# Two PSUM banks for the scan's diagonal, the cb tiles in SBUF, and TensorE's program written out for both layers

## The chip, the core and the metric

One core of one Trainium2 chip runs the whole kernel in a single launch. The time is device microseconds from start to end; the median of several executions counts. In the profile PE is TensorE's matmuls and PEld its weight loads, DVE is VectorE, ACT is ScalarE, POOL is GpSimd and SP is SyncE, which here only starts DMAs. A "q" behind an engine (DVEq) is its sequencer: drains, waits, register work.

## What is computed

An encoder of two layers on 256 tokens of width 1024, float32. The reference, cut down:

```python
for i in range(DEPTH):                       # DEPTH = 2
    h = rms_norm(x, mix_norm_g[i])
    proj = h @ w_in[i]                       # q, k, v, z, xBC, dt, memory q, 3 gates
    y_da  = diff_attention(q, k, v, ...)     # 8 heads
    y_ssm = mamba2_bidir(z, xBC, dt, ...)    # 32 heads, 4 groups, forward and backward scan
    y_xa  = mem_cross_attention(xq, rms_norm(mem), w_mem_kv[i])
    merged = g0 * (y_da @ wb_da) + g1 * (y_ssm @ wb_ssm) + g2 * (y_xa @ wb_xa)
    x = x + merged @ w_out[i]
    h = rms_norm(x, ffn_norm_g[i])
    gate, up = split(h @ w_ffn_in[i])
    x = x + (silu(gate) * up) @ w_ffn_out[i]
return rms_norm(x, final_norm_g)

# one direction of the scan, chunks of 128 tokens:
cb = einsum('bclgn,bcsgn->bcgls', Cc, Bc)                 # per group
m = cb * segsum_exp(a)                                    # decay between tokens
y_diag = einsum('bcgrls,bcsgrp->bclgrp', m, xdt)          # inside a chunk
y_off  = einsum(Cc, state of the other chunk) * exp(a_cs) # between chunks
```

## The kernel before

**Weights in units.** All large matrices stream through one ring of four slots. A unit is 128 x 1024 numbers of a weight (two blocks of 128 rows, 512 columns); a layer has 220 of them, numbered 0 to 219, and `GROUPS` lists to which product each group of units belongs. Every number is split into a high part and a rest, so that fast float32r matmuls give float32 results. For each unit SP loads `w_raw`, ScalarE casts the high part `wH` (line 896), VectorE, or for some units GpSimd, forms `wL` = `w_raw` - `wH` (line 1258, or 1191), and TensorE makes 12 to 24 matmuls from it (line 596), into the banks PS0 and PS1. An engine's step for unit u casts unit u + 3; so the operands of a unit are asked for three units ahead. While the input projections run ("mixing", units 26 to 125) all `wL` are VectorE's.

**Side work.** Everything else (norms, attention, convolution, scan) is cut into small steps. `layer_plan` gives each a unit number and an engine; `each_step` writes, for every engine, unit 0, its steps, unit 1, its steps and so on. Every engine runs its own list in order and meets the others at semaphores alone. The small matmuls and transposes write four side banks S0 to S3 of PSUM. `take(lay, bank)` makes TensorE wait until the bank's last reader has added to `side_free[bank]`; `side_uses` holds how often a layer takes each bank. TensorE can do nothing for the next unit while a side step waits.

**The scan.** 16 ticks i (4 groups g x 2 chunks c x 2 halves of the heads). The names and where they stand, x being the unit of tick i, 67 + 3i in the first layer's numbering:

- `conv`, `conv_silu`: convolution on VectorE (lines 1476, 1482), silu on ScalarE (1079), per block of 512 channels; `xs_turn` (TensorE, 797) transposes the result into bank 3, `xs_copy` (ScalarE, 1084) takes it out and frees the bank.
- `cb` (TensorE): B and C of group g, 256 x 256 numbers, into bank g % 2. `cb_rows` (ScalarE, 1107) copies the middle 256 columns of 512, the blocks between different chunks, to SBUF as `cboff`. The two diagonal blocks stay in the bank.
- `diff` (VectorE, 1544 and 1546) at x - 2, `decay_exp` (ScalarE, 1110) at x, `decay` (VectorE, 1554) at x + 3: the decay times cb's diagonal block, read from the bank. The last of four frees it.
- `diag` (TensorE) at x + 6: the tick's product, into bank 2. A chunk k has two ticks; the first takes the bank.
- `weigh`, `skip` (GpSimd, 1205 and 1213), `off` (TensorE, bank 3, reads `cboff`).
- `join` (VectorE): off's bank 3 times a gain (1564), plus diag's bank 2 (1567), and its drain (1568) frees bank 2. It stands one unit ahead of the diag of the next chunk. `gated` (1572, 1577) finishes the chunk in SBUF.
- `ssm_norm`, `ssm_turn` (TensorE, 854), `ssm_high` (ScalarE, 1124), `ssm_low` (VectorE, 1266): norm and transpose of the result; the first five transposes use bank 0.

Ahead of the scan come `dt_sums` (sums of dt by TensorE, which need VectorE's `aL`), the second half of the attention heads (`da_scores`, `da_exp`, `da_combine`, `da_turn`, line 769, and so on) and `cb_prod` (VectorE, 1526) with `cb_diag` (TensorE, sixteen matmuls of one column a layer in the trace) for the skip gain.

**Loops.** Each engine's program for a layer stands in one loop over both layers, and eight of its feed-forward groups in an inner loop. For TensorE this is

```python
            with pe.Fori(0, DEPTH) as lay:
```

at line 864; with `lay` in a register, each semaphore value it waits for is computed by register instructions.

## Time and profile before

| | |
|---|---|
| median of 3 executions | 1512.65 us (1511.44 to 1516.13) |
| profiled execution, its own time | 1514.97 us |
| its span, first to last instruction | 1513.1 us |
| TensorE matmuls, weight loads | busy 95%, 85% |
| VectorE, ScalarE, GpSimd | busy 63%, 53%, 24% |
| granted TensorE clock, mean | 0.986 of full |
| chain that ended last | TensorE 70%, VectorE 13%, its sequencer 8%, ScalarE 4% |

A busy TensorE here means matmuls that overlap: one of 512 columns is shown with 389 ns, and they start 227 ns apart. So the share says little on how much can be gained; the stops do, and the clock. Each view below is of this one execution. Layer 1 lasts to 760 us, layer 2 to some 1500 us, and the scan of layer 1 lies between about 264 and 475 us.

### The profile page before, as it was taken

The numbers are of one execution on the slowest core, as the hardware profiler recorded it, in microseconds if no ns is written. First come the engines' busy times: TensorE is split into PE (matmuls) and PEld (weight loads), VectorE is DVE, ScalarE is ACT, GpSimd is POOL, SyncE is SP. The second block draws the span as 40 slices with busy tenths as digits, with TensorE's granted clock in tenths as the row PEclk, the third lists the DMA queues.
The fourth block names the chain that finished last, engine by engine and source line by source line (L and its number), as shares of the span: only waits on it lengthen the run. The fifth ranks groups of instructions, "written<-read, shape, count | busy, mean of one in ns | idle before, by whom it ended". The sixth has DMA issues, their size and how long they took to land.

```text
span 1513.1 us, 25594 instructions
## 1 busy us (share of the span) xinstructions
PE 1443.5 (95%) x8905; PEld 1285.0 (85%) x8921; DVE 950.1 (63%) x1294; ACT 807.5 (53%) x1221; POOL 363.7 (24%) x170
## 2 busy tenths in 40 slices
PE   5999999999899999999999999999998999999997
PEld 5899888877777889999889988878786778899986
DVE  5354756989987446654433447588899864565543
ACT  5455577655555446444444546756556454544444
POOL 2310000110113344445333000001110134444443
PEclk9999999999999999999999999999999999999999
DMA  6564444665655564656555544446665556556564
GB/s 211 169 173 132 121 129 123 182 194 170 179 182 165 174 190 150 194 186 221 177 173 150 160 124 124 126 128 208 187 187 166 166 170 183 167 179 190 173 227 149
DMA packets 158500, 255.55 MB, mean 169 GB/s; under 512 B 12729, under 2 KB 58923, under 8 KB 158379
## 3 DMA queue, kind: packets, MB, share of 16 engines
q1 hardware_dynamic: 156427, 252.41, 55.3%
q10 hardware_dynamic: 1952, 1.61, 0.3%
q8 instruction: 66, 1.08, 0.3%
q14 instruction: 55, 0.45, 0.1%
HBM read 252.80 MB, written 1.18 MB: 168 GB/s over the span
## 4 chain that ended last, share of the span: by engine, by line
PE 70%; DVE 13%; DVEq 8%; ACT 4%; issue 3%; ACTq 1%; DMA 1%
PE PS L596 62%; PE S L596 6%; DVE wL L1258 5%; DVEq L1545 2%; DVEq L1479 2%; ACT wH L896 1%; PE S L603 1%; DVE actLf L1482 1%; DVE regA L1546 1%; DVEq L1558 1%; DVE regA L1544 1%; ACT scr L1045 1%; DVE regA L1554 1%; DVE scr L1567 1%; DMA rows<-in_ssm_D_dram 1%
## 5 line engine op out<-in xcount | busy, mean ns | idle before, releaser
L896 ACT CAST wH<-w_raw 128x1024 fp32r<-128x1024 f32 x443 | 458.2, 1042 | 550.6 <-PE PS L596 541.4
L1258 DVE TENSOR_TENSOR wL<-w_raw,wH 128x1024 fp32r<-128x1024 f32 (+1 forms) x322 | 438.3, 1363 | 406.4 <-ACT wH L896 392.1
L596 PE MATMUL PS<-hH,wH 128*128 128x256 f32 x1472 | 423.4, 288 | 0.0
L596 PE MATMUL PS<-hH,wL 128*128 128x256 f32 x1472 | 418.1, 284 | 0.0
L596 PE MATMUL PS<-hL,wH 128*128 128x256 f32 x1472 | 418.1, 284 | 0.0
L1191 POOL TENSOR_TENSOR wL<-w_raw,wH 128x1024 fp32r<-128x1024 f32 (+1 forms) x121 | 304.9, 2520 | 415.4 <-ACT wH L896 415.0
L596 PEld LDWEIGHTS PS<-hH,wH 128*128 128x128 f32 x1472 | 284.1, 193 | 4.3 <-issue 4.0
L596 PEld LDWEIGHTS PS<-hL,wH 128*128 128x128 f32 x1472 | 284.1, 193 | 0.3
L596 PEld LDWEIGHTS PS<-hH,wL 128*128 128x128 f32 x1472 | 283.9, 193 | 0.0
L596 PE MATMUL PS<-wH,actH 128*128 128x512 f32 x560 | 223.5, 399 | 0.0
L596 PE MATMUL PS<-wL,actH 128*128 128x512 f32 x560 | 219.2, 391 | 0.0
L596 PE MATMUL PS<-wH,actL 128*128 128x512 f32 x560 | 219.1, 391 | 0.0
L596 PE MATMUL PS<-wH,hH 128*128 128x512 f32 (+1 forms) x416 | 165.9, 399 | 0.0
L596 PE MATMUL PS<-wL,hH 128*128 128x512 f32 (+1 forms) x416 | 160.0, 385 | 0.0
L596 PE MATMUL PS<-wH,hL 128*128 128x512 f32 (+1 forms) x416 | 159.9, 384 | 0.0
L1205 POOL TENSOR_TENSOR regA<-actHf,dts 128x512 f32<-128x512 f32 x8 | 9.5, 1191 | 603.0 <-ACTq L1085 603.0
L596 PEld LDWEIGHTS PS<-wL,actH 128*128 128x128 f32 x560 | 105.7, 189 | 22.8
L596 PEld LDWEIGHTS PS<-wH,actL 128*128 128x128 f32 x560 | 106.0, 189 | 20.9
L596 PEld LDWEIGHTS PS<-wH,actH 128*128 128x128 f32 x560 | 106.0, 189 | 20.8
L596 PEld LDWEIGHTS PS<-wL,hH 128*128 128x128 f32 x416 | 79.3, 191 | 16.0
L596 PEld LDWEIGHTS PS<-wH,hH 128*128 128x128 f32 x416 | 79.6, 191 | 15.2 <-issue 1.3
L596 PEld LDWEIGHTS PS<-wH,hL 128*128 128x128 f32 x416 | 79.5, 191 | 14.2
(239 smaller groups left out, 1561.0 us busy)
## 6 DMA issues: line engine op xcount, KB each, us to landing
w_raw<-in_w_in_dram SPq DMA_DIRECT2D x192, 512.0 KB
w_raw<-in_w_ffn_in_dram SPq DMA_DIRECT2D x176, 256.0 KB
w_raw<-in_w_branch_dram SPq DMA_DIRECT2D x64, 512.0 KB
w_raw<-in_w_ffn_out_dram SPq DMA_DIRECT2D x44, 512.0 KB
w_raw<-in_w_mem_kv_dram SPq DMA_DIRECT2D x35, 512.0 KB
regA<-cs_rows SPq DMA_DIRECT2D x64, 256.0 KB, 4.5
w_raw<-in_w_out_dram SPq DMA_DIRECT2D x16, 512.0 KB
regA<-in_mem_dram SPq DMA_DIRECT2D x6, 512.0 KB, 5.4
```

The lines of the kernel that those rows point to most:

```text
L596: return nc.tensor.matmul(o, l, r, start=first, stop=last, skip_group_check=True)
L603: ins = nc.tensor.transpose(dst[:, at:at + P], src(t, k), ident[:, :])
L896: nc.scalar.copy(wH[:, slot].rearrange("p k c -> p (k c)")[:, q], raw[:, slot].rearrange("p k c -> p (k c)")[:, q]).then_inc(h_done[slot], 1)
L1045: ins = nc.scalar.activation(sc[b][:, T * q:T * (q + 1)], S[q // 2][:, T * (q % 2):T * (q % 2 + 1)], ACT.Exp, bias=nmx[b][:, q:q + 1], sca ...
L1191: nc.gpsimd.tensor_tensor(wL[:, slot].rearrange("p k c -> p (k c)")[:, q], raw[:, slot].rearrange("p k c -> p (k c)")[:, q], wH[:, slot].r ...
L1258: v.tensor_tensor(wL[:, slot].rearrange("p k c -> p (k c)")[:, q], raw[:, slot].rearrange("p k c -> p (k c)")[:, q], wH[:, slot].rearrange ...
L1479: dve.drain()
L1482: ins = v.scalar_tensor_tensor(tile[:, j, :], cin[:, j, k:k + T], p_cw[:, q:q + 1], tile[:, j, :], ALU.mult, ALU.add)
L1544: v.tensor_tensor(side, side, gains(cs[:, q:q + 4], 4, P), ALU.subtract)
L1545: dve.drain()
L1546: v.copy_predicated(b, upR[:, :].bitcast(U32).unsqueeze(1).broadcast_to([P, 4, P]), f)
L1554: ins = v.tensor_tensor(e, e, S[g % 2][:, (T + P) * c:(T + P) * c + P].unsqueeze(1).broadcast_to([P, 4, P]), ALU.mult)
```

## The change

1. TensorE's loop over the layers is a Python loop: its program stands there twice (6849 rows of instructions where there were 3658), with semaphore values as constants. The inner feed-forward loop stays, and so do the layer loops of the other engines.
2. `diag` takes banks 2 and 1 in turn, chunk by chunk.
3. `cb` takes bank 0 only; `cb_rows` copies all 512 columns to SBUF, drains and frees the bank. `decay` and `off` read that copy. The two copies lie in `scr` where `yN[0]` was; the tile `cboff` is gone.
4. `xs_turn` uses bank 0 instead of 3.
5. The plan's numbers: `dt_sums` to `cs_base` one unit later; attention heads 4 to 7 one unit earlier; `cb_diag` two units behind `cb_prod` instead of one; the scan's ticks one unit later; `xs_turn` two units apart and one or more later; `ssm_turn` 0 to 3 at ticks 41, 43, 45, 47 instead of 37, 39, 41, 43, counted from a start that is itself one later.

```diff
-    put(u + 6, "pe", "dt_sums")
+    put(u + 7, "pe", "dt_sums")
...
-        u = (first("xbc", 4) + 1 if half == 0 else first("v", 1) + 2) + 3 * j
+        u = (first("xbc", 4) + 1 if half == 0 else first("v", 1) + 1) + 3 * j
...
-    x = [first("xbc", 0) + 9 + 3 * i for i in range(4 * SG)]
-    u = first("xbc", 5) + 10
+    x = [first("xbc", 0) + 10 + 3 * i for i in range(4 * SG)]
+    u = first("xbc", 5) + 11
     put(u, "dve", "cb_prod")
-    put(u + 1, "pe", "cb_diag")
+    put(u + 2, "pe", "cb_diag")
...
-    for r, (turn, split) in enumerate(((37, 38), (39, 40), (41, 42), (43, 44), (59, 60), (59, 61), (60, 62), (60, 63))):
+    for r, (turn, split) in enumerate(((41, 42), (43, 44), (45, 46), (47, 48), (59, 60), (59, 61), (60, 62), (60, 63))):
...
-                put(u + 5 + (b == 0) + t, "pe", "xs_turn", 2 * b + t)
-                put(u + 6 + (b == 0) + t, "act", "xs_copy", 2 * b + t)
+                put(u + 6 + 2 * t, "pe", "xs_turn", 2 * b + t)
+                put(u + 7 + 2 * t, "act", "xs_copy", 2 * b + t)
...
-        cboff = [v3(t, NT) for t in (scr[:, 6144:6400], cboff_t[:, :])]
+        cb = [scr[:, 2560:3072], scr[:, 3072:3584]]
...
                 elif kind == "xs_turn":
-                    take(lay, 3)
+                    take(lay, 0)
...
                 elif kind == "cb":
-                    take(lay, i % 2)
+                    take(lay, 0)
...
                 elif kind == "diag":
                     g, c, hf = tick(i)
+                    bank = 2 - i // 2 % 2
                     if hf == 0:
-                        take(lay, 2)
+                        take(lay, bank)
...
-            with pe.Fori(0, DEPTH) as lay:
+            for lay in range(DEPTH):
...
                 elif kind == "cb_rows":
                     if i >= 2:
                         act.wait_ge(off_done, 8 * lay + 2 * i - 2)
-                    nc.scalar.copy(cboff[i % 2], v3(S[i % 2][:, P:P + T], 2)).then_inc(cb_ready, 1)
+                        act.wait_ge(m_done, 16 * lay + 4 * i - 4)
+                    nc.scalar.copy(cb[i % 2], S[0][:, :]).then_inc(side_free[0], 1)
+                    act.drain().then_inc(cb_ready, 1)
...
-                    ins = v.tensor_tensor(e, e, S[g % 2][:, (T + P) * c:(T + P) * c + P].unsqueeze(1).broadcast_to([P, 4, P]),
-                                          ALU.mult)
-                    if i % 4 == 3:
-                        ins.then_inc(side_free[g % 2], 1)
+                    v.tensor_tensor(e, e, cb[g % 2][:, (T + P) * c:(T + P) * c + P].unsqueeze(1).broadcast_to([P, 4, P]),
+                                    ALU.mult)
```

Two places show how this moves instructions. The names in square brackets are the semaphores waited for. First TensorE in the first layer, behind unit 103, at diag 10, before (`ssm_m` says that decay 10 is done) and after:

```order
2259 L592 REGISTER_ALU
2260 L842 REGISTER_ALU [waits xs_ready,side_free2]
2261 L596 MATMUL S<-actHf,regA 128x64 [waits ssm_m]
2262 L596 MATMUL S<-actHf,regA 128x64 x3
2263 L664 REGISTER_ALU
2264 L596 MATMUL PS<-wH,actH 128x512 [waits l_done0]
```

```order
2125 L595 MATMUL PS<-wL,actH 128x512
2126 L595 MATMUL S<-actHf,regA 128x64 [waits ssm_m,xs_ready,side_free1]
2127 L595 MATMUL S<-actHf,regA 128x64 x3
2128 L595 MATMUL PS<-wH,actH 128x512 [waits l_done1]
2129 L595 MATMUL PS<-wH,actL 128x512
```

The product now waits for the bank of two chunks ago, a unit later in the plan (the next unit's slot is 1, not 0), and the register instructions are gone.

Second VectorE, its units 111 to 114 in the first layer. Each `wL` row opens a unit; L1266 with `ssm_gh` is an ssm_low, L1554 a decay, L1564 with L1567 a join, L1326 the sum of a branch. Before:

```order
471 L1258 TENSOR_TENSOR wL<-w_raw,wH 128x1024 [waits h_done2]
472 L1266 SCALAR_TENSOR_TENSOR actL<-S,lp,actH 128x128 [waits ssm_gh]
473 L1266 SCALAR_TENSOR_TENSOR actL<-S,lp,actH 128x128 x3
474 L1258 TENSOR_TENSOR wL<-w_raw,wH 128x1024 [waits h_done3]
475 L1552 REGISTER_ALU
476 L1554 TENSOR_TENSOR regA<-regA,S 128x512 [waits ssm_exp]
477 L1257 REGISTER_ALU
478 L1258 TENSOR_TENSOR wL<-w_raw,wH 128x1024 [waits h_done0]
479 L1318 REGISTER_ALU
480 L1326 SCALAR_TENSOR_TENSOR scr<-scr,PS 128x1024 [waits unit_used1,psum_free1]
481 L1258 TENSOR_TENSOR wL<-w_raw,wH 128x1024 [waits h_done1]
482 L1564 TENSOR_TENSOR scr<-S,dts 128x512 [waits ssm_off]
```

And after, the lines counted one higher:

```order
468 L1259 TENSOR_TENSOR wL<-w_raw,wH 128x1024 [waits h_done3]
469 L1267 SCALAR_TENSOR_TENSOR actL<-S,lp,actH 128x128 [waits ssm_gh]
470 L1267 SCALAR_TENSOR_TENSOR actL<-S,lp,actH 128x128 x3
471 L1258 REGISTER_ALU
472 L1259 TENSOR_TENSOR wL<-w_raw,wH 128x1024 [waits h_done0]
473 L1319 REGISTER_ALU
474 L1327 SCALAR_TENSOR_TENSOR scr<-scr,PS 128x1024 [waits unit_used1,psum_free1]
475 L1553 REGISTER_ALU
476 L1555 TENSOR_TENSOR regA<-regA,scr 128x512 [waits ssm_exp]
477 L1259 TENSOR_TENSOR wL<-w_raw,wH 128x1024 [waits h_done1]
478 L1267 SCALAR_TENSOR_TENSOR actL<-S,lp,actH 128x128 [waits ssm_gh]
479 L1267 SCALAR_TENSOR_TENSOR actL<-S,lp,actH 128x128 x3
```

Decay 14 has moved behind the branch's sum, from unit 112 to 113, and reads `scr` instead of S; the join of unit 114 has given its place to the third ssm_low, which stood at unit 109, and follows one unit later.

## Rows read from the trace of the kernel before

**Rows 1.** The page: busy tenths of VectorE in 40 slices

```profile
DVE  5354756989987446654433447588899864565543
```

**Rows 2.** Writers of S, layer 1: what ended TensorE's idle time, us, times

```profile
  DVEq L1568: 9.9, 4
  ACT actHf L1084: 2.9, 4
  DVEq L1451: 2.2, 2
  DVEq L1587: 1.5, 1
  DVE aL L1265: 1.0, 1
  DVE regA L1526: 0.8, 1
```

**Rows 3.** The same view, layer 2, 830:1255 us: its largest difference from layer 1

```profile
  DVEq L1451: 2.3, 2
```

**Rows 4.** Timeline of TensorE: start us, us, work, idle before

```profile
265.58 0.63 PE L769 MATMUL S<-ident,scr 128*128 128x128 f32 x4 [1.65 <-DVEq L1451]
...
412.26 0.43 PE L596 MATMUL S<-actHf,regA 128*128 128x64 f32 x2 [4.75 <-DVEq L1568]
...
457.34 0.43 PE L596 MATMUL S<-actHf,regA 128*128 128x64 f32 x2 [1.07 <-DVEq L1568]
...
762.72 0.38 PE L596 MATMUL PS<-actH,wH 128*128 128x256 f32 x1 [2.06 <-issue]
```

**Rows 5.** Instructions of line 864: duration ns min/median/max, first and last start

```profile
L864 PEldq COMPARE_BRANCH  x2: 78/2918/5758, 756.5 to 1499.8; - x2
```

**Rows 6.** Stretches: busy us (x) of each engine, PEclk, DMA share, GB/s

```profile
268.00:274.00 6.00, 6.00 (x25) 4.97 (x25) 5.61 (x11) 0.37 (x1) 0.00 (x0) 0.72 0.53 141
...
411.00:418.00 7.00, 5.73 (x22) 4.62 (x23) 6.10 (x11) 1.21 (x2) 0.00 (x0) 0.76 0.40 107
763.00:769.00 6.00, 6.00 (x40) 6.00 (x40) 0.85 (x1) 3.22 (x9) 2.08 (x1) 0.72 0.50 162
1152.00:1161.00 9.00, 5.48 (x19) 4.75 (x20) 8.21 (x13) 2.27 (x2) 0.00 (x0) 0.62 0.27 76
```

**Rows 7.** Groups of VectorE, 264:449 us: busy, mean ns, idle before, releasers

```profile
L1258 DVE TENSOR_TENSOR wL<-w_raw,wH 128x1024 fp32r<-128x1024 f32 x50 | 63.7, 1276 | 12.8 <-ACT wH L896 8.2 <-issue 1.8
```

**Rows 8.** Timeline of ScalarE and VectorE at the scan's door

```profile
259.25 1.28 ACT L1079 ACT_TABLE_LOAD   x1
260.55 1.06 ACT L1079 ACTIVATE regA<-regA 128x1024 f32<-128x1024 f32 x1
...
262.84 1.23 DVE L1258 TENSOR_TENSOR wL<-w_raw,wH 128x1024 fp32r<-128x1024 f32 x1 [4.53 <-ACT wH L896]
```

**Rows 9.** Timeline of VectorE around ends of its units

```profile
414.24 1.22 DVE L1258 TENSOR_TENSOR wL<-w_raw,wH 128x1024 fp32r<-128x1024 f32 x1
...
444.80 1.12 DVE L1266 SCALAR_TENSOR_TENSOR actL<-S,lp,actH 128x128 fp32r<-128x128 f32 x4
...
450.95 1.22 DVE L1326 SCALAR_TENSOR_TENSOR scr<-scr,PS 128x1024 f32<-128x1024 f32 x1 [1.65 <-PE PS L596]
452.31 3.47 DVE L1258 TENSOR_TENSOR wL<-w_raw,wH 128x1024 fp32r<-128x1024 f32 x1
455.70 0.68 DVE L1564 TENSOR_TENSOR scr<-S,dts 128x512 f32<-128x512 f32 x1
...
457.30 1.45 DVE L1258 TENSOR_TENSOR wL<-w_raw,wH 128x1024 fp32r<-128x1024 f32 x1
...
1200.58 1.46 DVE L1258 TENSOR_TENSOR wL<-w_raw,wH 128x1024 fp32r<-128x1024 f32 x1
```

**Rows 10.** Instructions of lines 1554 and 1572: duration ns min/median/max

```profile
L1554 DVE TENSOR_TENSOR regA<-regA,S x32: 674/685/690, 289.9 to 1203.6; 128x512 f32<-128x512 f32 x32
...
L1572 DVE TENSOR_TENSOR scr<-scr x16: 676/685/2933, 323.4 to 1221.4; 128x512 f32<-128x512 f32 x16
```

More of the change, by code:

```diff
@@ L140, in layer_plan @@
     put(u + 5, "dve", "dt_out")
-    put(u + 6, "pe", "dt_sums")
-    put(u + 7, "dve", "dt_cs")
-    put(u + 8, "pe", "cs_turn")
-    put(u + 9, "act", "dt_decay")
-    put(u + 9, "dve", "dt_wgt")
-    put(u + 10, "act", "cs_store")
-    put(u + 11, "dve", "cs_base")
+    put(u + 7, "pe", "dt_sums")
+    put(u + 8, "dve", "dt_cs")
+    put(u + 9, "pe", "cs_turn")
+    put(u + 10, "act", "dt_decay")
+    put(u + 10, "dve", "dt_wgt")
+    put(u + 11, "act", "cs_store")
+    put(u + 12, "dve", "cs_base")
     for h in range(XH):
@@ L177, in layer_plan @@
                 put(u + 11 + 2 * q, "dve", "da_low", 2 * half + q)
-    x = [first("xbc", 0) + 9 + 3 * i for i in range(4 * SG)]
-    u = first("xbc", 5) + 10
+    x = [first("xbc", 0) + 10 + 3 * i for i in range(4 * SG)]
+    u = first("xbc", 5) + 11
     put(u, "dve", "cb_prod")
-    put(u + 1, "pe", "cb_diag")
-    put(u + 2, "dve", "d_gain")
+    put(u + 2, "pe", "cb_diag")
+    put(u + 3, "dve", "d_gain")
     for g in range(SG):
@@ L209, in layer_plan @@
     for n, b in enumerate(CONV_ORDER):
-        u = first("xbc", b) + (4 if b == 5 else 6 if b == 0 else 5)
+        u = first("xbc", b) + (4 if b == 5 else 7 if b == 0 else 5)
         for q in range(4):
@@ L257, in pool_splits @@
     return u % 2 == 1 and not mixing
-SIDE_USES = [23, 20, 33, 28]
+SIDE_USES = [33, 22, 29, 20]
 PAR_LOADS, ROW_LOADS = 7, 7
@@ L295, in build @@
         upR, loR, onesR = (sb(n, P, F32R) for n in ("upR", "loR", "onesR"))
-        cboff_t = sb("cboff", T)
         cs_rows = nc.dram_tensor("cs_rows", (NT, 2 * SH, P), F32, kind="Internal").ap()
@@ L796, in step @@
                     for j in range(4):
-                        ins = nc.tensor.transpose(S[3][:, P * j:P * (j + 1)], conv_tile(n)[:, j, P * t:P * (t + 1)],
+                        ins = nc.tensor.transpose(S[0][:, P * j:P * (j + 1)], conv_tile(n)[:, j, P * t:P * (t + 1)],
                                                   ident[:, :])
@@ L827, in step @@
                     for c in range(NT):
-                        ins = mm(S[i % 2][:, T * c:T * (c + 1)], BT[:, i, P * c:P * (c + 1)], CT[:, i, :], True, True)
+                        ins = mm(S[0][:, T * c:T * (c + 1)], BT[:, i, P * c:P * (c + 1)], CT[:, i, :], True, True)
                     ins.then_inc(cb_done, 1)
@@ L834, in step @@
                     pe.wait_ge(cb_ready, SG * lay + i // 2 + 1)
-                    mm(S[3][:, :], cboff[i // 2 % 2][:, 1 - c, :], xw[i % 2], True, True).then_inc(off_done, 1)
+                    mm(S[3][:, :], cb[i // 2 % 2][:, P * (2 - c):P * (3 - c)], xw[i % 2], True, True).then_inc(off_done, 1)
                 elif kind == "diag":
                     g, c, hf = tick(i)
+                    bank = 2 - i // 2 % 2
                     if hf == 0:
-                        take(lay, 2)
-                    if hf == 0:
+                        take(lay, bank)
                         pe.wait_ge(xs_ready, 8 * lay + 2 * g + c + 1)
@@ L844, in step @@
                         h = 4 * hf + j
-                        ins = mm(S[2][:, DH * h:DH * (h + 1)], RB[i % len(RB)][:, j, :],
+                        ins = mm(S[bank][:, DH * h:DH * (h + 1)], RB[i % len(RB)][:, j, :],
                                  xsN[g][:, c, DH * h:DH * (h + 1)], h == 0, True)
@@ L1083, in step @@
                     act.wait_ge(xs_turned, 8 * lay + i + 1)
-                    nc.scalar.copy(xsN[b][:, t, :], S[3][:, :]).then_inc(side_free[3], 1)
+                    nc.scalar.copy(xsN[b][:, t, :], S[0][:, :]).then_inc(side_free[0], 1)
                     act.drain().then_inc(xs_ready, 1)
@@ L1550, in step @@
                     if i % 4 == 0:
-                        dve.wait_ge(cb_done, SG * lay + g + 1)
+                        dve.wait_ge(cb_ready, SG * lay + g + 1)
                     dve.wait_ge(exp_done, 16 * lay + i + 1)
                     e = RB[i % len(RB)]
-                    ins = v.tensor_tensor(e, e, S[g % 2][:, (T + P) * c:(T + P) * c + P].unsqueeze(1).broadcast_to([P, 4, P]),
-                                          ALU.mult)
-                    if i % 4 == 3:
-                        ins.then_inc(side_free[g % 2], 1)
+                    v.tensor_tensor(e, e, cb[g % 2][:, (T + P) * c:(T + P) * c + P].unsqueeze(1).broadcast_to([P, 4, P]),
+                                    ALU.mult)
                     dve.drain().then_inc(m_done, 1)
@@ L1566, in step @@
                     dve.wait_ge(diag_done, 16 * lay + 2 * i + 2)
-                    v.tensor_tensor(ytmp, ytmp, S[2][:, :], ALU.add)
-                    dve.drain().then_inc(side_free[2], 1)
+                    bank = 2 - i % 2
+                    v.tensor_tensor(ytmp, ytmp, S[bank][:, :], ALU.add)
+                    dve.drain().then_inc(side_free[bank], 1)
                 elif kind == "gated":
```

## The prediction

> **What bounds the kernel now.** TensorE is busy in nine tenths of nearly every slice, so I read first why it stops at all. The view of the instructions that write the side banks S, one layer at a time, says what its idle time in front of them ended on: 18.7 us per layer, of which 9.9 us in four waits for VectorE's join (line 1568) and 2.9 us in four waits for ScalarE's copy out of bank 3 (line 1084) [rows 2, 3]. One wait stands outside the layers: 2.06 us that ended on nothing but issue [rows 4], at the branch of the layer loop. That branch row lasts 5.8 us where it is taken and 0.08 us where it falls through [rows 5].
>
> Second, the granted clock. Several stops are followed by a stretch at 1.2 GHz. A stretch costs its length times what is missing from full clock: 6 x 0.28 = 1.7 us at 268:274, 7 x 0.24 = 1.7 us at 411:418, 6 x 0.28 = 1.7 us at 763:769, 9 x 0.38 = 3.4 us at 1152:1161 [rows 6]. Layer 1 has three such stretches behind side work (the third, at 319:325, like the first), layer 2 has two, both like the last.
>
> Third, who is late where TensorE waits. VectorE's tenths in slices 8 to 12 are 9, 8, 9, 9, 8 [rows 1]; from 264 to 449 us its largest group waited only 8.2 us for ScalarE's halves, 4.5 of them in the first wait [rows 7]. What VectorE does not fill with counted work there are drains behind its own instructions. So in the scan TensorE waits for an engine that has no rest itself. The waits can be taken away; the time of VectorE can't.
>
> **The change, part by part.** I count in units: a layer has 220 weight units, TensorE takes about 2.9 us for one, and each engine's side steps hang behind its unit. A shift is how much earlier TensorE finishes a unit than before.
>
> *Layer loop written out.* The 2.06 us go [rows 4], and so does the slow stretch behind them, 1.7 us [rows 6]: 3.8 us, once. The casts for the next layer's first three units are ordered before the loop's end on ScalarE and VectorE, so TensorE's operands are there; ScalarE, VectorE and GpSimd keep their own loops. Register instructions run ahead of queued matmuls and are worth nothing.
> The Trainium skill, Runtime: NRT & Kernel Launch, section Instruction fetch mechanics, says that a taken branch to far code stalls until its block is fetched, and that straight code streams; the trace agrees with its 5.8 us row.
>
> *Ahead of the scan.* dt_sums one unit later: 1.0 us goes [rows 2], since VectorE's aL is late by that and a unit is 2.9 us. The second half of the attention heads starts a unit earlier, so that da_turn waits 2.2 us less (two waits, the one before the scan 1.65 us [rows 4]), and cb_diag stands two units behind cb_prod instead of one: 0.8 us less [rows 2]. The slow stretch at 268:274 followed just these, with sixteen one-column matmuls in between; now they lie in three places, so I drop its 1.7 us.
>
> *Two banks for diag, and bank 0 for the transposes xs_turn.* The diagonal product of chunk k needed bank 2, which join k-1 frees one unit before; with banks 2 and 1 in turn it needs join k-2. Its other wait, for decay, stands three units back in both orders. So the 9.9 us lose their cause. xs_turn no longer meets off and da_out in bank 3: 2.9 us lose theirs [rows 2].
>
> *cb in SBUF.* cb_rows copies 512 columns instead of 256, four times a layer. 1024 elements take ScalarE 1.06 us [rows 8], so 256 more are some 0.27 us, 1.1 us per layer on an engine that is busy 53% of the span: nothing. decay reads SBUF instead of PSUM: line 1554 (with S) takes 685 ns, line 1572 (SBUF alone, same size) 685 ns [rows 10]: nothing.
> The Trainium skill, VectorE: DVE Perf Modes, section The TRN2 errata, gives a PSUM source 62 cycles more than an SBUF source, which as an estimate would make 16 decays a layer 1.0 us cheaper in all. The rows show no difference, and they decide.
>
> *What TensorE would gain if nothing else were late.* Up to the end of unit 115 of layer 1: 9.9 + 2.9 + 2.2 + 1.0 + 0.8 = 16.8, less the 1.07 us of the last diag wait, which lies behind unit 115 [rows 4], gives 15.7; with three slow stretches 5.1: a shift of 20.8 us.
>
> *What VectorE allows.* Steps of the scan now stand mostly one unit later, and ssm_turn 0 to 3 five units later, on one bank: each needs the ssm_low before it, on VectorE. I take the last, ssm_turn 3 behind unit 115, which needs ssm_low 2, the last step of VectorE's unit 114. In the trace VectorE ends its unit 114 at 457.30 us and TensorE its unit 115 at 457.34 - 1.07 = 456.27 us [rows 4, 9]. Four things bring VectorE there sooner:
> - it starts sooner with TensorE: 1.0 + 0.6 = 1.6 us (dt_sums, and the first da_turn wait, 2.2 less 1.65);
> - its wait of 4.53 us at 262.84. ScalarE was then behind with attention's exp and after it silu with its table load, 1.28 + 1.06 us [rows 8]; with exp one unit earlier the casts follow at once. I take 4.0;
> - its small waits up to unit 114: 8.2 - 4.5 = 3.7 us [rows 7] and 1.65 us for TensorE itself at 450.95 [rows 9]: 5.3 us, which an earlier TensorE takes away;
> - work that the new order puts behind that point: a join, 457.30 - 455.70 = 1.6 us, and one ssm_low, 1.3 us with its drain [rows 9]: 2.9 us.
>
> Sum 13.8 us, so VectorE is there at 443.5 us, and TensorE can't pass before: shift 456.27 - 443.5 = 12.8 us, not 20.8. Behind it the wait of 1.07 us goes, since decay 14 is long done: 13.8 us for the layer. The remaining 8.0 us turn into other waits for VectorE. The first to be seen is xs_turn 6: its convolution ends at 414.24 us [rows 9], sooner by 1.6 + 4.0 + 3.7 and a join, 10.9, so at 403.3, and silu adds 2.4 [rows 8]: 405.7 us. TensorE ended unit 103 at 412.26 - 4.75 = 407.5 [rows 4]; 20.8 less this wait, its slow stretch and what comes later leaves some 14 us of shift, and diag and two units more make 400 us. The slow stretches that such waits may bring are paid from the same 8.0 us. The wait for n_done, 1.5 us [rows 2], keeps its distances and stays.
>
> Layer 2 has the same groups of waits, none more than 0.1 us apart from layer 1 [rows 2, 3], and VectorE's unit 114 ends at 1200.58 us against TensorE's 1199.5: the same 13.8 us.
>
> Sum: 2 x 13.8 + 3.8 = 31.4 us. The profiled execution took 1514.97 us (span 1513.1), 2.3 us over the median of 1512.65. 1514.97 - 31.4 = 1483.6; from the median it would be 1481.3. I say **1484 us**.
>
> **The rivals.**
> (a) *VectorE does not bind*, because what binds in my sum is spread better than I reckon, or its drains shrink when nobody collides. Then the full 20.8 + 1.07 us go in layer 1, and 23.6 in layer 2 (its two slow stretches are 6.8 instead of 5.1): 45.5 + 3.8 = 49.3, so 1466 us. For it: VectorE had up to three units of lead in casts. Against it: nine tenths busy for 185 us.
> (b) *VectorE binds harder.* ScalarE's detour at 262 us stays, 4.0 us a layer, and ssm_turn 1 to 3 each lose 1 us more in the round over bank 0 (turn, ssm_high, ssm_low, next turn). Per layer 13.8 - 4.0 - 3.0 = 6.8: 13.6 + 3.8 = 17.4, so 1498 us. The two halves decide separately, and either alone gives 1490 to 1492.
> (c) *Slower.* GpSimd and VectorE hold each other up when both read SBUF. A wL of otherwise 1.2 us lasted 3.47 at 452.31 us [rows 9], where GpSimd added two SBUF tiles, and line 1572 has one of 2.93 us [rows 10]. decay was spared as long as it read PSUM. If each of the 32 decays now lost 2.24 us, VectorE, the bound, would be 72 us longer, and the time 1484 + 72 = 1556 us. It decides from 31.4 / 32 = 1.0 us per decay. Against it: line 1572 has two SBUF inputs in the same stage and a median of 685 ns; in the scan GpSimd has just sixteen operations a layer (weigh and skip).
> The Trainium skill, SBUF — State Buffer, section Who interferes with whom, has this rule: a VectorE instruction with two SBUF inputs contends with a GpSimd instruction that reads SBUF, one with a PSUM input doesn't. The trace agrees with its long rows.
> (d) *No change to speak of*: every wait comes back elsewhere, as 2 x 13.8 us of new waits on VectorE, and only the branch's 3.8 us remain: 1511 us.
>
> **How the numbers follow.** Forecast (1476 to 1493) 0.60; (a) 0.13; (b) 0.19; (c) 0.03; (d) 0.05. The range for 8 in 10 reaches a little into (a) and takes in (b): 1472 to 1501. What a measurement can tell from no change is about 0.3%, 4.5 us: faster means under 1508. Faster 0.60 + 0.13 + 0.19 = 0.92; the same 0.05; slower 0.03.
>
> **What would show it.** In the profile after: no idle time and no long branch row at the layer's end, and clock 1.00 behind it; no wait for line 1568's join in front of diag; VectorE busy for nine tenths over a stage that is some 13 us shorter; TensorE's idle time in front of S now ended by ssm_low (line 1266 before) or silu's transposes, 2 to 5 us each around units 105 to 115; decay at 685 ns. I am wrong on VectorE if those waits are missing and the time is near 1466; wrong on ScalarE's detour if VectorE's wait of 4.5 us is still there; wrong on the price of SBUF if decay's mean is over 900 ns.

## Result and the profile after

The changed kernel takes 1503.81 us (median of 4 executions, 1503.17 to 1504.74), beside 1512.5 us of the kernel before in the same comparison: a ratio of 0.9939, 95% interval [0.9924, 0.9954]. It is faster by some 9 us, where 31 us had been forecast. The profiled execution of the changed kernel took 1503.9 us, its span 1502.0 us. The mean granted clock is 0.986, as before.

The page after, busy tenths of VectorE and granted clock in 40 slices (before: [rows 1]):

```profile
DVE  5354757999997446554434446689999863565543
...
PEclk9999999999989999999999999999999999999999
```

Slices 8 to 12 were 9, 8, 9, 9, 8 and are 9 throughout. The next view is that of [rows 2] and [rows 3], what TensorE's idle time in front of the writers of S ended on, first layer 1, then layer 2 (825:1250 us):

```profile
  ACTq L1079: 8.2, 3
  DVE actL L1267: 2.8, 2
  ACT actLf L1061: 2.2, 1
```

```profile
  ACTq L1079: 8.1, 3
  DVE actL L1267: 3.7, 2
  ACT actLf L1061: 2.2, 1
```

All that [rows 2] named is gone: no join, no bank 3, no aL, no cb_prod; n_done waits no more either. In their place stand silu (for xs_turn), ssm_low (for ssm_turn) and, in front of the weight matmuls, wL: 3.0 us in layer 1. From 18.7 us a layer it has become 16.2 us in layer 1. The longest new waits, in TensorE's timeline (start, us, work, idle before), and the start of layer 2, which answers to the last row of [rows 4]:

```profile
414.17 1.09 PE L796 MATMUL S<-ident,actLf 128*128 128x128 f32 x4 [4.35 <-ACTq L1079]
...
439.79 1.11 PE L853 MATMUL S<-ident,regB 128*128 128x128 f32 x4 [2.63 <-DVE actL L1267]
...
756.63 0.28 PE L595 MATMUL PS<-actH,wH 128*128 128x256 f32 x1
```

xs_turn 6 starts at 414.17 us where the forecast had silu's end at 405.7. The convolution before it ends at 413.0 us, only 1.2 us sooner than the 414.24 of [rows 9], where 10.9 had been forecast; so VectorE is already late here. Behind both waits the clock falls (stretches as in [rows 6]; PEclk is the third number from the end), and it is full at the layer's end:

```profile
411.00:419.00 8.00, 4.83 (x14) 3.99 (x15) 7.24 (x11) 5.49 (x7) 0.00 (x0) 0.59 0.29 80
439.00:444.00 5.00, 4.21 (x14) 3.55 (x15) 4.67 (x8) 1.14 (x4) 0.00 (x0) 0.66 0.38 134
755.00:762.00 7.00, 7.00 (x53) 6.69 (x53) 2.45 (x2) 4.83 (x11) 2.41 (x1) 1.00 0.58 175
```

Where the 11.1 us between the two spans come from can be read from TensorE's position at the same work in both traces. At the first norm_turn it is 0.5 us ahead. At the end of layer 1 (its last matmul ends at 760.66 us before and 756.8 after) it is 3.9 us ahead. At the first norm_turn of layer 2 it is 7.7 us ahead (784.5 us before, 776.8 after). A slow stretch around 815 us, half as long after (clock 0.72 over 12 us before, 0.86 after), adds 1.5, and the whole rest of layer 2 adds 1.9. Inside layer 1 TensorE had been much further ahead: where the kernel before stands at 401.7 us it leads by 8 us, and at the end of unit 115 by 1.2 us. The row of norm_turn (ns, first and last start) and the stretch of the slow clock, before and after:

```profile
L603 PE MATMUL S<-ident,regB x16: 270/272/273, 784.5 to 794.5; 128*128 128x128 f32 x16
```

```profile
812.00:824.00 12.00, 12.00 (x79) 12.00 (x79) 2.20 (x4) 4.74 (x6) 4.73 (x2) 0.72 0.61 173
```

```profile
L602 PE MATMUL S<-ident,regB x16: 270/272/273, 776.8 to 786.8; 128*128 128x128 f32 x16
```

```profile
806.00:818.00 12.00, 12.00 (x91) 12.00 (x91) 4.82 (x8) 5.78 (x6) 4.12 (x3) 0.86 0.58 162
```

So between these two executions the layer loop gave its 3.8 us, and the layers 3.4 and 1.9 us where 13.8 each were forecast.

Now VectorE. Its groups from 264 to 449 us, the same view as [rows 7], of after:

```profile
L1259 DVE TENSOR_TENSOR wL<-w_raw,wH 128x1024 fp32r<-128x1024 f32 x49 | 61.5, 1263 | 6.8 <-ACT wH L895 2.7 <-issue 1.6
...
L1545 DVE TENSOR_TENSOR regA<-regA,dts 128x512 f32<-128x512 f32 x32 | 24.8, 816 | 0.7 <-issue 0.6
L1555 DVE TENSOR_TENSOR regA<-regA,scr 128x512 f32<-128x512 f32 x14 | 13.0, 926 | 1.4 <-issue 1.4
```

and the two of them that were quick before, of before:

```profile
L1544 DVE TENSOR_TENSOR regA<-regA,dts 128x512 f32<-128x512 f32 x32 | 23.1, 763 | 0.3 <-issue 0.2
...
L1554 DVE TENSOR_TENSOR regA<-regA,S 128x512 f32<-128x512 f32 x15 | 10.3, 683 | 1.4 <-issue 1.2 <-ACT regA L1110 0.2
```

decay took 683 ns and takes 926. Its median has hardly moved, though (line 1555, ns min/median/max, both layers):

```profile
L1555 DVE TENSOR_TENSOR regA<-regA,scr x32: 680/692/2849, 288.7 to 1196.9; 128x512 f32<-128x512 f32 x32
```

Ten of the 32 are long: eight of 1.5 us and two of 2.8 us, 11 us more than the median in all. VectorE and GpSimd around two of them:

```profile
331.49 1.53 DVE L1555 TENSOR_TENSOR regA<-regA,scr 128x512 f32<-128x512 f32 x1
...
449.03 2.84 DVE L1555 TENSOR_TENSOR regA<-regA,scr 128x512 f32<-128x512 f32 x1 [0.21 <-issue]
```

```profile
331.40 1.07 POOL L1206 TENSOR_TENSOR regA<-actHf,dts 128x512 f32<-128x512 f32 x1 [28.35 <-ACTq L1084]
332.44 1.49 POOL L1214 TENSOR_TENSOR scr<-actHf,dts 128x512 f32<-128x512 f32 x1
...
448.94 2.38 POOL L1235 TENSOR_TENSOR regB<-regB,scr 128x1024 f32<-128x1024 f32 x1 [18.86 <-DVEq L1330]
```

Each of the ten starts 0.08 to 0.09 us behind a GpSimd operation and ends 0.55 us behind its end (332.47 and 333.02, 451.32 and 451.87). I call this a collision. The two collisions of 2.8 us, with GpSimd's sum behind unit 113, are not new as such: in the kernel before the same sum met a wL, the one of 3.47 us [rows 9]. New are the eight of 1.5 us, 6.7 us in both layers.

### The profile page after: what moved, and what is told of

Same layout as the page of the kernel before. It is cut to its first block, busy times and chain, and to the rows that moved or that the text cites. A ratio compares the mean times of both kernels' runs of the same rounds, so it can differ in the third digit from the quotient of the medians.

```text
span 1502.0 us, 25223 instructions
## 1 busy us (share of the span) xinstructions
PE 1440.8 (96%) x8905; PEld 1283.8 (85%) x8921; DVE 958.2 (64%) x1294; ACT 814.5 (54%) x1225; POOL 365.6 (24%) x170
## 3 DMA queue, kind: packets, MB, share of 16 engines
q8 instruction: 62, 1.02, 0.3%
## 4 chain that ended last, share of the span: by engine, by line
PE 73%; DVE 13%; DVEq 8%; ACT 2%; issue 2%; ACTq 1%; DMA 1%
PE PS L595 65%; PE S L595 5%; DVE wL L1259 4%; DVEq L1546 2%; DVE regA L1555 1%; DVEq L1480 1%; DVE actLf L1483 1%; DVE regA L1545 1%; DVE regA L1547 1%; PE S L602 1%; DVEq L1557 1%; ACT wH L895 1%; DVEq L1324 1%; DMA rows<-in_ssm_D_dram 1%; DVE regB L1577 1%
```

## Experiments

In each comparison the kernel before ran on the same chip. "Less than after" compares a ratio with 0.9939; that ratio has an interval of its own of 2.3 us to each side. The **collision sum** is worked out from the traces: over layer 1's scan (262 to 457 us), the time of every VectorE instruction above the fastest quarter of its kind. It was 8.6 us before and is 14.2 us after. How the quarter is taken moves single sums by up to 0.7 us, and their differences by 0.3.

**One: the layer loop alone**, in the kernel before.

```
-            with pe.Fori(0, DEPTH) as lay:
+            for lay in range(DEPTH):
```

> The kernel before with one part of the change alone: TensorE's layer loop written out, its plan and banks as they were. The two traces differ by 5.35 us between the last unit of layer 1 and unit 20 of layer 2, where the forecast had 3.8 us (2.06 idle, 1.7 slow clock). Theory A, all of this is the branch's (its idle time, and more slow clock behind it than I counted): 5.4 us less than before, about 1507 us, and no idle time at the layer's end. Theory B, the forecast's term holds and the rest belongs to the new plan: 3.8 us less, about 1508.8 us. If the inner work of layer 2 loses again what it gets (VectorE sets the end of the scan), less than 2 us remain, 1511 us.

1509.52 us, ratio 0.9972 [0.9959, 0.9984]: 4.2 us less (2.4 to 6.2). The term of 3.8 us holds. Theory A's 5.4 us is within the interval too, and in the trace TensorE is that far ahead in early layer 2, but 2.7 us of it are left at the end: the mean clock of this execution is 0.984. That the loop always costs 3.8 us is not shown. From the last transposes of line 603 in layer 1 (they start at 725.9 us before) to the first norm_turn of layer 2 (784.5 us) TensorE takes 58.6 us before and 54.7 here, 3.9 less. But in the traces of the three other kernels that keep the loop (experiments two, three and nine) it takes 56.1 to 56.4 us: it idles 1.1, 1.1 and 1.4 us at the branch, and no slow stretch follows (clock 1.00). The row of experiment nine, beside the 2.06 us of [rows 4]:

```profile
760.61 0.38 PE L596 MATMUL PS<-actH,wH 128*128 128x256 f32 x1 [1.42 <-issue]
```

So in those traces the loop costs 1.4 to 1.7 us, and the rest of the 3.9 belongs to that one execution of the kernel before. The times say 2.4 to 6.2; which of the two is nearer the usual cost stays open.

**Two: cb in SBUF alone**, in the kernel before.

```
-                    nc.scalar.copy(cboff[i % 2], v3(S[i % 2][:, P:P + T], 2)).then_inc(cb_ready, 1)
+                    nc.scalar.copy(cb[i % 2], S[i % 2][:, :]).then_inc(side_free[i % 2], 1)
+                    act.drain().then_inc(cb_ready, 1)
...
-                    ins = v.tensor_tensor(e, e, S[g % 2][:, (T + P) * c:(T + P) * c + P].unsqueeze(1).broadcast_to([P, 4, P]),
+                    v.tensor_tensor(e, e, cb[g % 2][:, (T + P) * c:(T + P) * c + P].unsqueeze(1).broadcast_to([P, 4, P]),
```

> The kernel before with another part alone: cb copied whole to SBUF, decay reads that copy, banks and plan as they were (a bank is then freed by ScalarE's copy instead of the last decay). In the changed kernel ten of the 32 decays last 1.5 to 2.9 us, each beside a GpSimd operation, 11 us in all. Theory A, that is the price of the second SBUF input, and VectorE sets the scan's pace: the decays beside GpSimd lengthen here too, their mean goes from 0.68 to about 1.0 us, and the time rises by 5 to 11 us, to 1517 to 1523 us. Theory B, the long decays come from the new order of the steps and not from the input: mean 0.69 us, time 1512.5 us within 1 us. My forecast's term for it was nothing.

1522.03 us, ratio 1.0063 [1.0046, 1.0081]: 9.5 us slower. Eight of 32 decays are long, 6.8 us in all; the mean in this stretch is 865 ns.

```profile
L1555 DVE TENSOR_TENSOR regA<-regA,scr 128x512 f32<-128x512 f32 x14 | 12.1, 865 | 1.4 <-issue 1.2 <-ACT regA L1111 0.2
```

VectorE and GpSimd of this kernel show who sets up the collision:

```profile
346.81 0.69 DVE L1576 TENSOR_TENSOR regB<-regB,scr 128x512 f32<-128x512 f32 x1
347.70 1.51 DVE L1555 TENSOR_TENSOR regA<-regA,scr 128x512 f32<-128x512 f32 x1 [0.19 <-issue]
```

```profile
347.62 1.04 POOL L1214 TENSOR_TENSOR scr<-actHf,dts 128x512 f32<-128x512 f32 x1 [8.00 <-DVEq L1577]
```

skip waits for y_done, which VectorE gives at the end of gated, and the next thing in VectorE's list is a decay. The collision is written into the order of steps; the bank input had kept it harmless. Theory A in its mechanism, though the mean of decay (0.865 us) is less than its 1.0. The rise in time is not explained in full by it. VectorE's other instructions collide less here, so that the collision sum rises only by 1.3 us in layer 1 and 1.8 in layer 2, and TensorE's waits for join by 3.5 us in both (11.3 and 12.0, from 9.9 each). The rest goes with the clock, 0.983 in the median of its executions (0.979 in the profiled one) where the kernel before has 0.986. What share the longer copy on ScalarE has in it was not tested.

**Three and four: less work for VectorE**, in the kernel before and in the changed one. The last tap of the convolution is left out for the x blocks, so the output is another.

```
-                    for k in (3, 4) if late else (1, 2):
+                    for k in ((3,) if n >= 2 else (3, 4)) if late else (1, 2):
```

> The kernel before with less work for VectorE in the scan: the last tap of the convolution is left out for the four x blocks, sixteen instructions of 0.48 us per layer, 7.7 us (the result is another, the rest of the program is the same). It shows what VectorE's length is worth in the kernel before. Theory A, VectorE sets the pace in both kernels, the join waits of 9.9 us per layer are only how it shows: 8 to 15 us less, 1498 to 1504 us. Theory B, the join waits are a matter of how far the steps stand apart in the plan: under 4 us less, above 1508 us.

> The changed kernel with the same sixteen convolution instructions per layer left out, 7.7 us of VectorE's work per layer. Theory A, VectorE's work sets the scan's end, since its steps have no rest: the waits for silu, ssm_low and wL shrink with it, 10 to 18 us less than the changed kernel, 1486 to 1494 us. Theory B, the distances in the plan (transposes one unit behind silu, ssm_turn one unit behind ssm_low) and the slow clock set it: at most 4 us less, 1500 us or more. If both hold in part, the wait for silu goes (8.2 us per layer now) and the wait for ssm_low (2.6 and 3.5 us) stays.

Of the 15.4 us of both layers, 8.2 us show in the kernel before (1504.18 us, 0.9946 [0.9928, 0.9965]) and 13.3 in the changed one (1490.06 us, 0.9851 [0.9833, 0.9870]). Theory A twice. Silu's waits fell to 5.9 us a layer and did not go; ssm_low's are 3.5 and 2.4 us, where they were 2.8 and 3.7. A microsecond of these taps is worth 0.5 us before and 0.9 after, by intervals of 0.3 to 0.7 and of some 0.6 to 1.1.

**Five: ssm_turn 0 to 3 later**, in the changed kernel.

```
-    for r, (turn, split) in enumerate(((41, 42), (43, 44), (45, 46), (47, 48), (59, 60), (59, 61), (60, 62), (60, 63))):
+    for r, (turn, split) in enumerate(((50, 51), (52, 53), (54, 55), (56, 57), (59, 60), (59, 61), (60, 62), (60, 63))):
```

> The changed kernel with ssm_turn, ssm_high and ssm_low 0 to 3 put behind the scan's crowded part: ticks 50, 52, 54, 56 instead of 41, 43, 45, 47 (units 118 to 124, where VectorE has some 5 us of lead in wL). TensorE's waits for ssm_low (2.6 us in layer 1, 3.5 in layer 2) and the slow stretches behind them (1.7 and 3.4 us) hang on VectorE's unit 110. Theory A, VectorE's work in the scan is the bound, so that 1.3 us per ssm_low taken out of it count: 8 to 12 us less than the changed kernel, 1492 to 1496 us. Theory B, TensorE is held at the same unit by the next thing that VectorE has late (decay 13 or 14, wL), and VectorE's total up to there has hardly changed: 0 to 4 us less, 1500 to 1504 us.

1499.53 us, ratio 0.9904 [0.9888, 0.9921]: 5.3 us less than after. Between the theories: the wait of 2.6 us for ssm_low and the slow stretch behind it went, and another of 1.7 us came. VectorE ends unit 114 at 450.2 us, 4.8 us sooner, for three ssm_low less.

**Six: diag in two banks, decay from the bank**, on top of five.

```
-        put(x[4 * g] - 2, "pe", "cb", g)
+        put(x[4 * g] + 1, "pe", "cb", g)
...
-        put(x[i] + 3, "dve", "decay", i)
+        put(x[i] + (2 if i % 4 == 3 else 3), "dve", "decay", i)
...
-                    v.tensor_tensor(e, e, cb[g % 2][:, (T + P) * c:(T + P) * c + P].unsqueeze(1).broadcast_to([P, 4, P]),
+                    ins = v.tensor_tensor(e, e, S[0][:, (T + P) * c:(T + P) * c + P].unsqueeze(1).broadcast_to([P, 4, P]),
```

> As the run with the late ssm_turn, and in addition decay reads cb's diagonal blocks from the bank again, with diag still in two banks: cb stays in bank 0 until the last decay of its group (placed one unit earlier) and the next cb is taken three units later; xs_turn uses bank 2, which is empty between two of its chunks; cb_rows copies 256 columns. Theory A, the second SBUF input costs what the first experiments showed (decays of 1.5 us beside GpSimd, 6.8 us in all and 9 us of time in the kernel before; 11 us of decays in the changed one): 8 to 12 us less than the run with the late ssm_turn alone. Theory B, two banks and the late steps have already used up what can be had, or the single bank for cb brings waits for decay 3, 7 and 11 of 2 to 4 us each: no less than that run, or more.

1502.94 us, ratio 0.9928 [0.9912, 0.9944]: 3.6 us more than five. Theory B. In layer 1 the collision sum falls by 4.4 us, to 10.5 us, less than decay's own share, since diff now meets GpSimd more often. But TensorE pays 11.6 us in layer 1 for the one bank of cb:

```profile
  DVE regA L1554: 11.6, 3
```

So the change bought two banks for diag with the copy of cb, and the copy had a price; but without it the waits only move to cb.

**Seven: xs_turn later**, on top of five.

```
-                put(u + 6 + 2 * t, "pe", "xs_turn", 2 * b + t)
-                put(u + 7 + 2 * t, "act", "xs_copy", 2 * b + t)
+                at = u + (8 + t if b else 6 + 2 * t)
+                put(at, "pe", "xs_turn", 2 * b + t)
+                put(at + 1, "act", "xs_copy", 2 * b + t)
```

> As the run with the late ssm_turn, and the transposes xs_turn of the last three x blocks stand three and four units behind their silu instead of one and three. TensorE's waits for silu, 8.2 us per layer in the changed kernel, were the first waits that the forecast named. Theory A, VectorE sets the pace of the whole stage: the waits come back in front of wL, decay or diag, and the time is within 3 us of the run with the late ssm_turn. Theory B, these waits are a matter of distance in the plan: they go and nothing takes their place, 10 to 16 us less than that run, slow stretches included.

1500.19 us, ratio 0.9900 [0.9882, 0.9918], the same as five. Theory A in its purest form: the waits for silu are gone, and in layer 1 this is what stands in front of PS instead (3.0 us after):

```profile
  DVE wL L1260: 9.3, 7
```

**Eight and nine: nearly no collisions**, in the changed kernel and in the kernel before. weigh and skip compute one column of 64 per head; the rest of their results is left out. GpSimd's sum behind unit 113 stays, and with it one collision a layer in both (a decay of 2.87 us, a wL of 3.47 us).

```
-                    nc.gpsimd.tensor_tensor(v3(xw[i % 2], HPG), v3(xsN[g][:, 1 - c, :], HPG),
+                    nc.gpsimd.tensor_tensor(v3(xw[i % 2], HPG)[:, :, 0:1], v3(xsN[g][:, 1 - c, :], HPG)[:, :, 0:1],
```

> The changed kernel with GpSimd's weigh and skip cut to one column of 64 per head (sixteen operations a layer of 8 elements instead of 512 per row; the rest of their results is left out, every wait is kept). It takes away what decay collides with, but for the one GpSimd sum at unit 113. Theory A, the collisions are the price of the second SBUF input: the decays of 1.5 us go to 0.69 us, 0.84 us for each of eight, and the time falls by 6 to 12 us, 1492 to 1498 us. Theory B, the time is set elsewhere: decays shorter, time within 2 us of the changed kernel's 1503.8.

> The kernel before with GpSimd's weigh and skip cut to one column of 64 per head, as was done to the changed kernel (1483.3 us, 20 us less; the rest of the two results is left out, every wait is kept). In the scan of the kernel before VectorE's instructions were 8.6 us per layer longer than their own shortest quarter, in the changed one 14.2 us. Theory A, what the collisions cost is what VectorE loses in them, and the kernel before had less of it because decay's bank input was spared: 8.6 x 2 less some that stays, at the smaller worth that VectorE's work had there (8.8 us for 15.4 us of taps), so 7 to 12 us less, about 1503 us; then the change without collisions is worth some 20 us, and 9 to 12 us of the missing gain are collisions. Theory B, the kernel before gains the same 20 us, to 1493 us: then the collisions explain nothing of the gain that is missing.

The changed kernel falls to 1483.31 us, ratio 0.9802 [0.9783, 0.9822], 20.7 us less than after. That is the mechanism of Theory A, but well over its 6 to 12 us. The kernel before falls to 1511.08 us, ratio 0.9984 [0.9972, 0.9997], 2.4 us less (0.5 to 4.2), which misses both theories (7 to 12 us, and 20). Between these two the whole change is worth 0.9802 / 0.9984 = 0.9818, 27.5 us (some 24 to 31), where with collisions it is worth 9.2. So two thirds of what it would bring is eaten by collisions. In layer 1 the collision sum fell by 5.1 us in the kernel before and by 10.8 in the changed one, to 3.5 and 3.4. Why the first is nearly free and the second costs all of it can be read from VectorE's wL group, 264:449 us, of the kernel before without collisions and of the changed kernel without them:

```profile
L1258 DVE TENSOR_TENSOR wL<-w_raw,wH 128x1024 fp32r<-128x1024 f32 x50 | 61.1, 1224 | 15.6 <-ACT wH L896 12.0 <-issue 1.2
```

```profile
L1259 DVE TENSOR_TENSOR wL<-w_raw,wH 128x1024 fp32r<-128x1024 f32 x52 | 63.3, 1223 | 8.1 <-ACT wH L895 3.8 <-issue 1.6
```

In the kernel before the wait for wH rises from 8.2 us [rows 7] to 12.0: of 5.1 us that VectorE saves, 3.8 become its own waiting, since the casts come no sooner than TensorE frees a slot (before, from 264 to 460 us, they wait for TensorE's matmuls 41 times, 71.8 us). In the changed kernel it rises from 2.7 to 3.8, and nearly all of the 10.8 us reach TensorE. Layer 2, counted between the same two wL, says the same: the wait rises from 3.4 to 8.1 us in the kernel before and stays in the changed one, 3.8 and 3.7.

Eight alone leaves a rival: GpSimd's results also come sooner in it. Ten answers that one, since there they come no sooner: on ScalarE a step of eight activations takes 2.0 us (14.1 us for seven of them, below), on GpSimd 1.0.

**Ten to twelve: weigh and skip on ScalarE**, with the full result; then, on top, ssm_turn later, and in twelve xs_turn later too.

```
+                    for h in range(HPG):
+                        ins = nc.scalar.activation(xw[i % 2][:, DH * h:DH * (h + 1)],
+                                                   xsN[g][:, 1 - c, DH * h:DH * (h + 1)], ACT.Copy,
+                                                   scale=wgt[:, q + h:q + h + 1])
```

> The changed kernel with weigh and skip done by ScalarE instead of GpSimd (eight activations with a scale per head, 128 x 64 each, in place of one multiplication; a step one unit later), the full result. Theory A, the collisions go as in the run with GpSimd's operations cut down, and ScalarE, busy 54% of the span, takes 16 times eight short activations, some 25 us per layer by the 0.37 us of its two to four hundred-element forms, beside TensorE: 14 to 20 us less than the changed kernel, 1484 to 1490 us. Theory B, ScalarE's casts then come late, since its steps stand ahead of them: waits for wH appear on VectorE and TensorE, and of the 20 us less than 10 stay, over 1494 us.

> As the run with weigh and skip on ScalarE, with ssm_turn 0 to 3 eight and more units later too. Theory A, VectorE is still the bound and 3.9 us of ssm_low per layer leave its crowded part: 4 to 6 us less again, as in the changed kernel (4.5 us), about 1480 us. Theory B, without the collisions VectorE is no longer what ends last there, or ScalarE is: within 2 us of the other run.

> As the run before, with xs_turn of the last three x blocks three and four units behind their silu. In the changed kernel this brought nothing, since VectorE's wL came next. Theory A, with VectorE relieved by the collisions the waits for silu (5.2 us per layer without weigh and skip) are a matter of distance for the most part: 3 to 8 us less. Theory B, VectorE is still as late as before with wL: within 2 us.

With weigh and skip on ScalarE: 1491.11 us, ratio 0.9848 [0.9833, 0.9863], 23 us faster than the kernel before and some 14 us faster than the changed one. It beats both, with the same output. The activations take 0.33 us each and overlap; 28 us of ScalarE's time up to 449 us in layer 1:

```profile
L1132 ACT ACTIVATE scr<-actHf,dts 128x64 f32<-128x64 f32 x56 | 14.1, 334 | 0.0
...
L1120 ACT ACTIVATE regA<-actHf,dts 128x64 f32<-128x64 f32 x32 | 8.1, 337 | 0.0
L1120 ACT ACTIVATE scr<-actHf,dts 128x64 f32<-128x64 f32 x24 | 6.0, 335 | 0.0
```

The collision sum is as small as in eight, some 3.4 us. The gain lies just under Theory A's 14 to 20. VectorE's wait for wH goes up to 9.0 us with it, so a part of Theory B is true as well: ScalarE's casts now come late at times, and of the 20.7 us 14 are had.

```profile
L1265 DVE TENSOR_TENSOR wL<-w_raw,wH 128x1024 fp32r<-128x1024 f32 x50 | 60.9, 1223 | 12.9 <-ACT wH L895 9.0 <-issue 1.4
```

The other two give 1493.64 us (0.9857 [0.9838, 0.9876]) and 1492.23 us (0.9853 [0.9835, 0.9871]), which can't be told from it: Theory B both times. TensorE's idle time in the trace is even 0.5 to 2 us less there. The profiled executions have a mean clock of 0.984 where the first has 0.990, but that is no difference between the kernels: over all executions the three have 0.986 to 0.990, 0.984 to 0.990 and 0.984 to 0.988.

## Why the prediction was wrong, step by step

**Right: the bound and the kind of the new waits.** The forecast said that VectorE sets the scan's end, and that TensorE would wait for silu and ssm_low, 2 to 5 us at a time around units 105 to 115. It waits 4.35 us behind unit 105 for silu and 2.63 us behind unit 111 for ssm_low. Three and four, and above all seven, show that VectorE's total counts for more than the distance of the steps. VectorE is busy for nine tenths, and no join stands in front of diag, as said. Rival (a) is out. The time lies 6 us from rival (b)'s 1498 and 7 from (d)'s 1511. Of (b) the half on ScalarE's detour came for the most part, as shown below. (d)'s reason is not borne out: the waits of the layers did not come back for want of anything to gain, since without the collisions the change is worth 27.5 us.

**Right: the layer loop**, 3.8 us, measured 4.2 (2.4 to 6.2). No idle time, clock 1.00. The slow stretch in it was that of one trace: in three other traces with the loop the whole comes to 1.4 to 1.7 us (experiment one), so its size is less sure than it looks. Register instructions are worth nothing, as said: from 529 to 726 us of the kernel before TensorE takes 196.9 us with them and 196.8 without (experiment one).

**Wrong: "decay reads SBUF instead of PSUM: nothing".** This is the step that failed. I priced it by the median of line 1572 in [rows 10], and the median was right again, 692 ns. What counted is who stands beside it: weigh starts with xs_copy and skip with the end of gated, both just ahead of a decay. The decays are 11 us longer in both layers, 0.35 us for each of the 32, 5.5 us a layer. The denser order adds 2.4 us a layer in the diffs, and the wLs lose 2.3 us less in collisions, so that the collision sum is up by 5.6 us a layer. Rival (c) had the mechanism and the rows, but asked only whether all 32 are hit; it put the turning point at 1.0 us and took 16 operations a layer for few. Of those 16, four hit decay in each layer, and GpSimd's sum behind unit 113 a fifth. The sign I had set for it, a mean over 900 ns, has come (926 in [rows 7]'s stretch, 1031 over all 32). The Trainium skill, SBUF — State Buffer, section Who interferes with whom, says that a VectorE instruction with two SBUF inputs contends with a GpSimd instruction that reads SBUF, and one with a PSUM input doesn't; two, eight and six agree with it in both directions (eight long decays of 32 with the SBUF input in two; none over 690 ns with the bank input in six; two of 32, both beside GpSimd's sum, in eight). The prediction named this rule and gave it 0.03, but only in its largest form, with every decay hit.

**Wrong in size: VectorE's sum.** VectorE was to end unit 114 at 443.5 us, 13.8 sooner. It ends it at 455.03, 2.3 sooner (the first two rows are its first waits, see below):

```profile
260.69 1.23 DVE L1259 TENSOR_TENSOR wL<-w_raw,wH 128x1024 fp32r<-128x1024 f32 x1 [1.92 <-ACT wH L895]
262.94 1.23 DVE L1259 TENSOR_TENSOR wL<-w_raw,wH 128x1024 fp32r<-128x1024 f32 x1 [1.02 <-ACT wH L895]
...
455.03 1.23 DVE L1259 TENSOR_TENSOR wL<-w_raw,wH 128x1024 fp32r<-128x1024 f32 x1
```

- *Sooner start and ScalarE's detour*, 1.6 + 4.0 = 5.6 us: 2.8 is what the other items leave for it, and its rows give 2.5. VectorE is 0.9 us sooner one wL ahead of the wait, and the wait of 4.53 us [rows 7, 8] has become two, of 1.92 and 1.02 us, 1.6 less: ScalarE's silu with its table load and two small steps still stand ahead of the cast. That half of rival (b) was right in part.
- *Small waits*, 5.3 us: measured 2.2. The waits for wH of this stretch went from 3.7 us (8.2 less 4.5) to 1.7 (2.7 less 1.0), that for TensorE from 1.65 to 0.45 us; other short stops, in front of join and of a wL, grew by 1.0.
- *Work moved behind*, 2.9 us: as reckoned.
- *Collisions*, 0: 5.6 us more.

2.8 + 2.2 + 2.9 - 5.6 = 2.3 us. From there the forecast's own rule goes on rightly: TensorE ends unit 115, at 455.1 us, at the time at which VectorE ends its unit 114, a shift of 1.2 us instead of 12.8. In the run without collisions VectorE ends that unit at 445.8 us, 11.5 sooner.

```profile
445.80 1.23 DVE L1259 TENSOR_TENSOR wL<-w_raw,wH 128x1024 fp32r<-128x1024 f32 x1
```

So with collisions away the sum of 13.8 would have been 2 us off; but there the collisions of the kernel before are away too, which hides that the first two items were 6 us too large. Both errors are there: without the two oversized items, 5.9 us a layer, I would have said some 1496 us, and with 5.6 us a layer for collisions some 1507. Of the 20.3 us that are missing in the profiled execution (31.4 less 11.1), the collisions are 11.2 and the two oversized items 11.8, so neither error alone explains it. The wait for n_done, 1.5 us a layer, which I said would stay, went. That leads to 1504.0 us, beside 1503.9 measured; so near only by luck, since layer 2 gave less than layer 1.

**Wrong: "TensorE waits for an engine that has no rest itself", for the kernel before.** VectorE did have rest there, 8.2 us of waits for wH, and what it gains in the kernel before can become more of it: nine brings 2.4 of some 11 us. ScalarE's casts have come closer to a limit of their own in the changed kernel, which the forecast did not ask about: from 264 to 460 us they wait 9.6 us for w_raw's DMA, where no such wait is listed before. That it costs time is not shown, as VectorE's waits for wH are fewer all the same.

**da_turn**: two waits of 2.2 us were to go. One is gone; the other is as long as both were, and ends on ScalarE's da_head (line 1061).

**The clock**: unchanged in the mean, 0.986, as new waits bring new slow stretches. I had paid these from the 8.0 us of waits that come back. **Layer 2** was taken as layer 1's copy, but gave 1.9 instead of 3.4 us: the wait for ssm_low is 0.9 us longer, and the slow stretch behind it longer too (1173:1181 us after, PEclk 0.57).

```profile
1173.00:1181.00 8.00, 6.42 (x19) 5.22 (x20) 6.82 (x14) 1.56 (x7) 0.00 (x0) 0.57 0.40 130
```

## What to carry to other kernels

When an operand moves from a bank to SBUF, don't price it by the median of a neighbour: list the GpSimd operations, see what releases each, and look which VectorE instruction starts right behind that event. Before taking an engine for the bound, look at its own waits: what they grow by is the part of its relief that does not arrive. How much that will be the waits of the kernel before don't say in advance. There the taps were worth 0.5 us and the collisions 0.2 us for each microsecond, in the same kernel: the waits for wH grew by 3.9 of 15.4 us in one case and by 8.5 of some 11 in the other. And one trace's slow stretch is not yet a price: look whether a second trace of the same code has it. And when two engines collide while a third is half idle, move the small work to the third.

## What was unexpected in the hardware's behaviour

A VectorE multiplication of 0.69 us beside a GpSimd operation does not become somewhat slower; it ends 0.55 us behind GpSimd's end, 1.53 us beside one that has 1.0 us to go and 2.84 us beside one with 2.3. GpSimd pays too: the multiplication of 1.04 us lasts 1.49 us when VectorE is in between. Who starts first matters: four other decays of the changed kernel also overlap with a weigh, but started ahead of it; they took 0.68 us, and the weigh 1.27 to 1.57 instead of 1.04. With a bank as one input the same 32 instructions had no row over 690 ns [rows 10]. And the mean granted clock differs between executions of one and the same kernel, from 0.983 to 0.988 in the kernel before (1517.14 and 1510.57 us) and from 0.984 to 0.990 with weigh and skip on ScalarE and a late ssm_turn. That is as large as most effects studied here, so one profiled execution can't settle a difference of a few microseconds.
